# Feed-forward's last three down units taken together, and the joins' transposes moved into the neighbouring products

## The reference

```
def rms_norm(x, g): y = xf * lax.rsqrt(jnp.mean(xf * xf, axis=-1, keepdims=True) + NORM_EPS); return y * g
def swiglu_ffn(h, w_gate, w_up, w_down): return (jax.nn.silu(h @ w_gate) * (h @ w_up)) @ w_down

# first block, layer l = 0, 1
x = x + 0.5 * swiglu_ffn(rms_norm(x, ffn1_norm[l]), ffn1_w_gate[l], ffn1_w_up[l], ffn1_w_down[l])
x = x + y                     # y: convolution, pooling and attention of rms_norm(x, mix_norm[l]), @ w_out[l]
x = x + 0.5 * swiglu_ffn(rms_norm(x, ffn2_norm[l]), ffn2_w_gate[l], ffn2_w_up[l], ffn2_w_down[l])
x = rms_norm(x, post_norm[l])

# second block, layer i = 0, 1
h = h + 0.5 * rms_norm_2(swiglu(rms_norm_2(h, g[0]), ffn_w13[i, 0], ffn_w2[i, 0]), g[1])
h = h + rms_norm_2(m, g[3])   # m: gated MLP (i = 0) or RWKV-7 (i = 1) of rms_norm_2(h, g[2])
h = h + 0.5 * rms_norm_2(swiglu(rms_norm_2(h, g[4]), ffn_w13[i, 1], ffn_w2[i, 1]), g[5])
h = h + rms_norm_2(gate * (p[i] @ ple_w_proj[i]), g[7])
```

## Time and profile before

| | |
|---|---|
| median of 3 runs | 2159.88 us (2158.36 to 2159.91) |
| the profiled execution | 2158.38 us, span 2156.6 us |
| PE busy | 2119.5 us, 98% of the span |
| PEld busy | 1804.0 us, 84% |
| DVE, ACT, POOL busy | 70%, 53%, 17% |
| mean granted PE clock | 0.998 |

### The profile page before, as it was taken

How to read it: one execution, slowest core, us unless ns; L and a number is a source line. 1 busy time by engine, 2 the same in 40 slices (tenths; PEclk the granted TensorE clock), 3 DMA queues, 4 the chain that set the end, 5 groups by cost and what they waited for, 6 DMA issues and landing times.

```text
span 2156.6 us, 39059 instructions
## 1 busy us (share of the span) xinstructions
PE 2119.5 (98%) x13578; PEld 1804.0 (84%) x13578; DVE 1519.8 (70%) x2382; ACT 1151.8 (53%) x1983; POOL 366.6 (17%) x462
## 2 busy tenths in 40 slices
PE   8999999999999999999999999999999999899998
PEld 7888888888888888888887988888888777778887
DVE  6666976667667966667667757667766778777666
ACT  5445754545546654555546546446644554455455
POOL 1111211112111211112110001111211112301111
PEclk9999999999999999999999999999999999999999
DMA  7655435555555346556556555556555442035653
GB/s 252 202 179 186 141 128 198 190 195 175 195 186 191 108 156 199 181 175 205 184 195 226 176 175 170 198 181 237 192 183 196 147 167 67 14 109 195 198 181 132
DMA packets 104254, 375.66 MB, mean 174 GB/s; under 512 B 11744, under 2 KB 12256, under 8 KB 104160
## 3 DMA queue, kind: packets, MB, share of 16 engines
q1 hardware_dynamic: 104160, 374.37, 51.9%
HBM read 373.28 MB, written 1.05 MB: 174 GB/s over the span
## 4 chain that ended last, share of the span: by engine, by line
PE 87%; DVE 6%; ACT 4%; issue 1%; POOL 1%; DMA 0%; SPq 0%; DVEq 0%; POOLq 0%; ACTq 0%
PE bank L938 27%; PE bank L942 14%; PE bank L187 13%; PE bank L188 13%; PE bank L189 13%; DVE w_lo L181 2%; ACT act L477 1%; PE bank L1221 1%; ACT w_hi L174 1%; DVE act L587 1%; PE bank L2209 0%; PE bank L2192 0%; PE bank L387 0%; ACT work L439 0%; PE bank L1187 0%
## 5 line engine op out<-in xcount | busy, mean ns | idle before, releaser
L938 PE MATMUL bank<-act,w_hi 128*128 128x512 f32 x2816 | 704.7, 392 | 3.4 <-DVE work L883 2.2
L938 PEld LDWEIGHTS bank<-act,w_hi 128*128 128x128 f32 x2816 | 515.1, 188 | 107.1 <-DVE act L587 3.8
L798 DVE TENSOR_TENSOR w_lo<-raw,w_hi 128x1024 fp32r<-128x1024 f32 x432 | 502.9, 1220 | 4.3 <-issue 1.0
L789 ACT ACTIVATE w_hi<-raw 128x1024 fp32r<-128x1024 f32 x432 | 424.9, 1050 | 2.3
L942 PEld LDWEIGHTS bank<-act,w_lo 128*128 128x128 f32 x2816 | 384.0, 190 | 27.7
L942 PE MATMUL bank<-act,w_lo 128*128 128x256 f32 x2816 | 392.5, 282 | 0.0
L889 DVE TENSOR_TENSOR work<-bank,work 128x256 f32<-128x256 f32 x176 | 74.8, 425 | 376.9 <-ACT work L819 376.9
L181 DVE TENSOR_TENSOR w_lo<-raw,w_hi 128x1024 fp32r<-128x1024 f32 x248 | 294.8, 1220 | 56.7 <-ACT w_hi L174 56.6
L850 POOL TENSOR_TENSOR work<-work,rb 128x256 f32<-128x256 f32 x176 | 130.0, 739 | 1037.3 <-DVE work L883 1037.3
L187 PE MATMUL bank<-w_hi,g_hi 128*128 128x512 f32 x704 | 277.0, 394 | 0.9 <-DVE w_lo L181 0.8
L188 PE MATMUL bank<-w_lo,g_hi 128*128 128x512 f32 x704 | 275.9, 392 | 0.0
(11 more groups left out here) (288 smaller groups left out, 2230.0 us busy)
## 6 DMA issues: line engine op xcount, KB each, us to landing
raw<-w_dram SPq DMA_DIRECT2D x680, 512.0 KB, 4.4
work<-rows_dram SPq DMA_DIRECT2D x13, 512.0 KB, 6.3
work<-rrows_dram SPq DMA_DIRECT2D x5, 512.0 KB, 3.5
x<-x_dram SPq DMA_DIRECT2D x2, 512.0 KB, 3.9
out<-x SPq DMA_DIRECT2D x4, 256.0 KB, 2.0
work<-g_dram SPq DMA_DIRECT2D x1, 640.0 KB, 9.7
work<-dist_dram SPq DMA_DIRECT2D x2, 256.0 KB, 4.6
work<-ws_dram SPq DMA_DIRECT2D x1, 512.0 KB, 8.1
```

What stands on the lines that cost most here:

```text
L789: nc.scalar.activation(c.w_hi[:, n % RING, :], c.raw[:, n % RING, :], ACT.Copy).then_inc(c.hi_ready, 1)
L798: nc.vector.tensor_tensor(c.w_lo[:, n % RING, :], c.raw[:, n % RING, :], c.w_hi[:, n % RING, :].bitcast(F32), ALU.subtract).then_inc(c.lo_ ...
L938: nc.tensor.matmul(bank[:, :], c.w_hi[:, slot(m), k * P:(k + 1) * P], c.act[:, k, :, :], start=k == 0, stop=False)
```

## The change

1. **Last down units.** PE's step 20 no longer takes down(19), nor does step 21 take down(20). After up(21) a new function takes down(19), down(20) and down(21) in two parts: first two of the four quarters of each unit, then the other two. The quarters follow the join's order: output half 0 of both token halves for the first block, token half 0 for the second block. The weights are stored in the new order (gate(21) and up(21) ahead of down(19)). Tile 21's `g_hi` and `g_lo` go to a spare tile of `act`, since the two `g` buffers are still in use.
2. **Turns.** In the `early` joins turns 1 and 2 stand between down(19) and down(20) of the second part (or in the mixer's last product, after its first token half); turns 3 and 4 stand in the next stage's first product, ahead of tile 2. DVE's list has the adds of half 0, tiles 0 to 3, the adds of half 1, tiles 4 to 7.
3. **Mixer entry.** The first two units are taken together: tiles 0 to 3 for both, then 4 to 7 for both.
4. **Token joins.** Adds and turns go by tokens, and one bank is replaced.
5. **Late feed-forward.** `spread_rows` moves from before to behind gate(2).

```
+def two_units(c, pe, n, out0, out1, there):
+    unit_there(c, pe, n + 1)
+    for half in (range(4), range(4, KT)):
+        for u, out in ((n, out0), (n + 1, out1)):
+            for k in half:
+                if u == n:
+                    there(pe, k)
...
+        self.by_token = row is not None and order is None and waiting > 0
+        self.adds = self.ROWS if self.by_token else self.QUADS
+        self.late_bank = 6 if plain is not None else 1
...
     def tensor(self, pe):
...
-        while self.turned < 4:
+        while self.turned < (2 if self.early else 4):
             self.turn(pe)
...
     def tile_there(self, pe, k):
+        if k >= 2 and self.early:
+            while self.turned < 4:
+                self.turn(pe)
...
+        if self.early:
+            self.first_half_vector(dve)
...
+    def last_downs(pe):
+
+        for part in range(2):
+            for n in range(3):
+                f, m = FT - 3 + n, count - 3 + n
+                if part == 0:
+                    unit_waited(pe, None, m)
+                    pe.wait_ge(s["gated_ready"].sem, s["gated_ready"].at(f + 1))
+                for t, h in out.order[2 * part:2 * part + 2]:
+                    last = down_quarter(f, m, t, h, end=n == 2)
+                    if n == 2 and (t, h) != out.order[3]:
+                        last.then_inc(quad.sem, 1)
+                if part == 1:
+                    last.then_inc(c.unit_used, 1)
+                    if n == 0 and out.early:
+                        out.turn(pe)
+                        out.turn(pe)
 
     def pe_step(pe, i, t):
...
-        if t >= 1:
+        if 1 <= t < FT - 2:
             add_down(pe, i, t - 1, m + 2, begin=t == 1)
...
             hidden(pe, None, 3, up[1])
-            join.spread_rows(pe)
             pe.wait_ge(s["gate_made"].sem, s["gate_made"].at(1))
             hidden(pe, None, 4, gate[0])
+            join.spread_rows(pe)
             pe.wait_ge(s["product"].sem, s["product"].at(1))
             hidden(pe, None, 5, up[0])
...
-        product_b(c, pe, first, c.bank[a_bank[0]], join.tile_there)
-        product_b(c, pe, first + 1, c.bank[gate_bank[0]])
+        two_units(c, pe, first, c.bank[a_bank[0]], c.bank[gate_bank[0]], join.tile_there)
...
-        product(pe, 7, 1, 3)
+        product(pe, 7, 1, 3, None, early_turns)
...
+    out[-4:-1] = out[-3:-1] + out[-4:-3]
     return out + [down[(FT - 1) * P:, :]]
```

More of the change, by code:

```diff
@@ L209, in product_b @@
     last.then_inc(c.unit_used, 1)
+def two_units(c, pe, n, out0, out1, there):
[5 more added lines that the diff above has]
+                    there(pe, k)
+                w = slice(k * P, (k + 1) * P)
+                last = three_products(c.nc, out[:, 0:S], c.w_hi[:, u % RING, w], c.w_lo[:, u % RING, w],
+                                      c.act_hi[:, k, :], c.act_lo[:, k, :], k == 0, k == KT - 1)
+            if half.stop == KT:
+                last.then_inc(c.unit_used, 1)
 def product_t(c, n, k, count, outs, t, tile0):
@@ L355, in tile @@
         at = (k // 2 % 2) * S
-        return self.c.bank[self.PLACE[k]][:, at:at + S]
+        bank = self.late_bank if self.by_token and self.PLACE[k] == 2 else self.PLACE[k]
+        return self.c.bank[bank][:, at:at + S]
     def gain_of(self, k):
@@ L379, in turn @@
         c, s = self.c, self.s
-        t, h = self.QUADS[self.turned]
+        t, h = self.adds[self.turned]
         self.turned += 1
@@ L433, in square @@
         parts, squares = (self.y_parts, s["y_squares"]) if self.post is not None else (self.parts, s["squares"])
-        t, h = self.QUADS[i]
+        t, h = self.adds[i]
         if self.start:
@@ L473, in high @@
         if k % 4 == 0:
-            act.wait_ge(s["turned"].sem, s["turned"].at(2 + k // 2))
+            act.wait_ge(s["turned"].sem, s["turned"].at((3 if self.by_token else 2) + k // (4 if self.by_token else 2)))
         if k >= 2:
@@ L618, in vector @@
                 self.add_y(dve)
+                if self.by_token:
+                    self.add_y(dve)
+        if self.early:
+            self.first_half_vector(dve)
         if not self.start:
@@ L759, in gate_unit, with hidden_half @@
     def gate_unit(t):
-        return 3 * t - 1 if t else 0
+        return 3 * t - 1 - (t == FT - 1) if t else 0
+    def hidden_half(f):
+        if f == FT - 1:
+            return c.act_hi[:, 2 * KT - 1, :], c.act_lo[:, 2 * KT - 1, :]
+        return c.g_hi[:, f % 2, :], c.g_lo[:, f % 2, :]
     def down_unit(f):
@@ L956, in down_quarter @@
         w, tok = slice(h * HALF, (h + 1) * HALF), slice(t * P, (t + 1) * P)
-        return three_products(nc, down[2 * t + h][:, :], c.g_hi[:, f % 2, tok], c.g_lo[:, f % 2, tok],
+        g_hi, g_lo = hidden_half(f)
+        return three_products(nc, down[2 * t + h][:, :], g_hi[:, tok], g_lo[:, tok],
                               c.w_hi[:, slot(m), w], c.w_lo[:, slot(m), w], begin, end)
@@ L1001, in tensor @@
             add_down(pe, None, 1, 7)
-            with pe.Fori(0, LOOPS) as i:
-                pe_step(pe, i, 3)
+            pe_step(pe, None, 3)
+            with pe.Fori(0, LOOPS - 1) as i:
                 pe_step(pe, i, 4)
+                pe_step(pe, i, 5)
         else:
@@ L1010, in tensor @@
                 pe_step(pe, i, 3)
-            pe_step(pe, None, FT - 2)
+        pe_step(pe, None, FT - 2)
         pe_step(pe, None, FT - 1)
[L1013 to L1021, removed]
+        last_downs(pe)
     return Stage(sync, scalar, vector, gpsimd, tensor)
@@ L1321, in tensor, with early_turns @@
         product(pe, 6, 0, 3, normed_there)
-        product(pe, 7, 1, 3)
+        product(pe, 7, 1, 3, None, early_turns)
+    def early_turns(pe):
+        out.turn(pe)
+        out.turn(pe)
     def evict(act, i):
```

9 lines of the change are left out of this document (5 added, 4 removed).

## The result

| | before | changed |
|---|---|---|
| median, us | 2159.26 (2158.36 to 2159.91, 4 runs) | 2172.38 (2171.91 to 2174.11, 4 runs) |
| profiled execution, us | 2158.38 | 2171.91 |
| its span, us | 2156.6 | 2170.0 |

The ratio is 1.0065 (95% interval 1.0053 to 1.0077): slower by 13 us. The direction is the forecast's. The median lies 0.6 us under the upper end of the range; by the ratio, the 2159.88 us that the prediction started from become 2173.9, just above that end. By the spans 13.45 us were lost, where the sum had 10.0: some 3.5 us of loss were not in it.

A forecast was written before the change was run, and what follows sets the result against it. PE, busy 98% of the span, was taken as the bound, so only its stand-stills count: 2 x (0.3 + 0.4 + 3.0 + 0 + 1.3) = +10.0; 2158.38 + 10.0 + 1.5 = 2169.9, stated as 2169.5 us, range 2163.5 to 2173.

The forecast's parts named there:

- Part 1: Last down units: PE waits for tile 21's g_lo ahead of down(21), +1.3 us in each of 8 feed-forwards.
- Parts 2 and 3: Mixer entry, twice, net +0.3 us each; FFN2 entry, twice, net +0.4 us each, with PE waiting 1.0 us before turn 3.
- Part 4: Post join and late feed-forward, twice: later spread_rows makes PE wait 2.9 us at down(0), plus 0.1 exposed spread; +3.0 us each.
- Both, and the clock falls: Rival, chance 0.12: one to three clock falls, likeliest at the late feed-forwards, add +1.7 to +5 us; 2171 to 2175.
- Part 5: Token joins, twice: 1.3 us won by token order, 1.3 lost to the stall; 0 each.
- Part 6: Ple joins, twice: PE stands still nowhere there, so the stall is paid in full; +1.3 us each.
- The 1.5 us added at the end: Added to the profile-based sum because the median of three runs, 2159.88 us, stood above the profiled 2158.38.

The follow-up runs named there:

- e7: Changed kernel with spread_rows back ahead of gate(2) and the third weight split of DVE's last step moved behind make_gated: 2155.76 us, ratio 0.9988.
- e8: Changed kernel with spread_rows back ahead of gate(2) and, in early joins, DVE's adds 3 and 4 between low tiles 1 and 2: 2161.75 us, ratio 1.0014.
- e1: Changed kernel with spread_rows put back ahead of gate(2) in the two late feed-forwards: 2163.84 us, ratio 1.0029.
- e5: Kernel before with one edit, the late feed-forward's spread_rows moved behind gate(2): 2167.61 us, ratio 1.0041.
- e9: Changed kernel with the token joins taken by output halves again (by_token False): 2172.54 us, ratio 1.007.
- e12: Changed kernel run once more, unaltered, for its profile: 2170.58 us in one run.
- e6: Changed kernel with spread_rows back ahead of gate(2), down(19)'s second half ahead of down(21)'s first, early turns behind down(20)'s second half: 2159.8 us, ratio 1.0003.
- e10: Changed kernel with spread_rows back, third split of DVE's last step behind make_gated, and adds 3 and 4 between low tiles 1 and 2: 2153.15 us, ratio 0.9977.
- e2: Changed kernel with useless filler matmuls ahead of down(0) in the two late feed-forwards, keeping PE busy: 2168.09 us, ratio 1.0042.
- e3: Changed kernel with one of the three weight splits of DVE's last step moved from ahead of add_gate(21) to just behind it: 2172.26 us, ratio 1.0063.

## Why the prediction came out as it did

- **Part 1, the stall: right.** 1.24 to 1.25 us eight times against 1.3; e7 shows its cause.
- **Parts 2 and 3, the entries: right,** +0.66 and +0.72 against 0.7 for the pair; +0.30 and +0.33 of it at the mixer entries (0.3 said), the rest at the FFN2 entries (0.4 said). The wait ahead of turn 3 there was 0.76 us instead of 1.0, and e8 shows that DVE's order made it.
- **Part 4: the step that failed,** by leaving the clock out of its sum. 3.0 said, 4.96 and 4.92 measured. The mechanism of the wait was right (e1, e5), and so was its size: 2.90 us by the starts (the row's 2.75, and 0.15 beyond the usual distance), and 0.14 for the exposed spread, against 2.9 and 0.1. Where the clock doesn't fall (e9's first late feed-forward, e12's second) the part costs 3.4. The 0.36 beyond those two terms are small: up(2) takes 0.10 longer, down(0) and down(1) behind the wait 0.18, and gate(2) starts 0.08 later. The other 1.5 is the clock, which the sum put at nothing. The prediction had this only as the rival "Both, and the clock falls", at 0.12. Its trace held the warning: a fall behind 0.98 us of idle and none behind 1.09. I read the second as a reason against, when the two together said that the length of the idle alone doesn't settle it, and a wait near three times as long deserved the larger chance. With 7 falls in 10 waits the term is 3.4 + 0.7 x 1.5 = 4.5 each, an estimate made afterwards: 3 us more in the sum.
- **Part 5, the token joins: wrong by half.** The sum was 1.3 won and 1.3 lost at each. At the RWKV mixer's the balance held (-0.02), but e9 gives only 0.63 of it to the order by tokens. At the gated MLP's only 0.65 was won, +0.60 left, and e9 gives none of it to that order. I had counted what is ahead of the last add; the first high tile waits for three of the four adds by tokens. In e9 it waits for two, of both tokens, and the first product came no sooner. What won the 0.65, and what keeps the rest, wasn't isolated.
- **Part 6, the ple joins: right,** +1.30 and +1.35 against 1.3, though such a stage moves by 0.2 to 0.3 with nothing edited in it (e5).
- **The 1.5 us added at the end** came from a median of three runs. The later medians of the kernel before, of 16 to 27 runs, are 2157.76 to 2158.51, near the profile's 2158.38; the changed kernel's median is 0.5 above its profiled execution. So the term hid some 1 us of the miss: that is luck.
- **The RWKV mixer,** given nothing, came out 0.8 us shorter: the fall of the earlier trace rows and its 1.7 us are missing from the changed kernel's profile, and other waits, not followed up, grew by 0.9. Falls in this mixer come and go between profiles (of the fourteen, the kernel before, e1 and e7 have one and e8 a longer one), and without one this stage still lies 0.3 us to 2.0 us under that of the kernel before in most, 0.1 to 0.4 above it in e9 and e6. So it isn't put down to the change. (The kernel before also shows the lower clock from 2151.8 us on, so the earlier trace rows isn't its only stretch; PE has no work left there, and it costs nothing.)

## What to carry to other kernels

When work is reordered on the busiest engine, the cover that it gave to a chain on other engines goes with it. Price each such chain from its own queue (here DVE's splits ahead of one add), and then look for what of that queue nobody waits for yet: with the spread back in its old place, moving one split and two adds turned +0.3% (e1) into -0.2% (e10). A new stand-still of TensorE of a few microseconds has to be priced with the clock as well, as a chance and a cost, not only as a rival.

## What the chip showed that I had not expected

- The clock falls or doesn't behind the same wait in the same program: 7 of 10 waits of 2.7 to 2.8 us, and in the kernel before once behind 0.98 us, not behind 1.09. Keeping PE busy over the wait with useless matmuls left no fall in e2's profile, and saved 1.5 us each.
- A multiply of POOL on 128x256 took 0.74 us alone and 1.65 beside a split of DVE that had started 0.16 us before it, in all eight feed-forwards of e3 (1.65 or 1.66); it ended 0.6 us behind the split. That is nearly as if it had waited for the split's end. The Trainium skill ("SBUF — State Buffer", section "SBUF: two separate sides") gives such a wait: the two engines share one pair of ports, which is "an exclusive lock", and an operation of DVE with two SBUF inputs shuts out one of GpSimd that reads there, for the whole instruction. By that rule, as an estimate, the multiply would have taken 186.02 + 1.22 - 186.18 + 0.74 = 1.80; the trace has 1.65. The lock itself no run here isolates.
